# Constant multiplications on TensorE in front of waits, at the seams of stages and between the steps of the norms

## The chip, the cores and the metric

One core of a Trainium2 chip runs the whole program. TensorE multiplies, VectorE, ScalarE and GpSimd (POOL in the profile) do the elementwise work, SyncE issues the DMAs. The metric is the device time of one execution in microseconds; the time of a kernel is the median of its runs.

## The reference

Sequence 512, model width 1024, float32. Two different blocks follow each other, each two layers deep:

```python
# first block, hybrid layer
h = rms_norm(x, g_mix)
z = h @ w_in                                        # latents, conv input, queries, keys, values, gates
o_a = mla_mixer(...); o_b = conv_mixer(...); o_c = nsa_mixer(...)
g_a, g_b, g_c = split(sigmoid(gate_mix))
x = x + (g_a * o_a + g_b * o_b + g_c * o_c) @ w_out
x = x + square(relu(rms_norm(x, g_ffn) @ w_ff1)) @ w_ff2          # 4096 wide
# second block, layer; sh1, sc1, g1, sh2, sc2, g2 = split(c @ mod_w + mod_b)
h = rmsnorm(x, norm1_g) * (1 + sc1) + sh1
x = x + g1 * mixer(h)      # sparse (top-k) attention and forgetting attention, each gated, then @ w_out
h = rmsnorm(x, norm2_g) * (1 + sc2) + sh2
x = x + g2 * conv_ffn(h)   # up to 2 x 2816, causal 3-tap conv, silu(a) * b, down
# and a last rmsnorm of the result
```

All eight heads of each attention see all 512 tokens under their masks.

## The kernel before

Activations lie transposed: features on the 128 partitions, the 512 tokens along the row, eight such tiles for a width of 1024. A weight chunk is 128 x 1024 float32; SyncE streams all of them through a ring in the order of use.

**Products.** Every linear product is exact to about float32 by splitting both sides into a high and a low part (`w_hi`, `w_lo`, `a_hi`, `a_lo`) that TensorE takes in a faster format, and adding three passes in one PSUM bank: high x high, high x low, low x high (`split_pass` L265, `split_products` L278). A pass over one unit of 128 output features is eight matmuls of 512 columns. ScalarE makes the high part of a chunk of weights (`weights_hi` L190), GpSimd its low part (`weights_lo` L213). At the start of a stage the source tiles are cut as well: ScalarE makes `a_hi` tile by tile and counts them in `src_hi` (`split_source_hi` L236), VectorE makes `a_lo` and counts in `src_lo` (`split_source_lo` L247). The first unit of such a stage is given the tuple `fresh`: in its first pass TensorE waits for `src_hi` before each of the eight matmuls, then does low weights x high source, and in its last pass waits for `src_lo` before each.

**Stages.** The program is a sequence of stages (`stage` L101). Each is a block of five instruction programs, one for each engine, with a barrier at its end that all engines meet; semaphores of the stage order the work inside it. PSUM has 8 banks of 128 x 512; nothing in PSUM is carried through a stage's end but the scale that a norm leaves in bank 7. Layer by layer:

- first block: `norm_stage`, `first_front_stage` (L1232), `head_norm_stage` (L1090), `attention_stage` (latent attention), `compressed_attention_stage` (L1688), `attention_stage` (two branches in one), `gate_stage` (L1817), `merge_stage` (L967), `linear_stage` for the output projection, `norm_stage`, `linear_stage` for `ff_up`, `down_stage`;
- second block: `norm_stage`, `front_stage` (L2100), `attention_stage` twice (sparse, forgetting), `gate_stage`, `merge_stage`, `linear_stage` for the output projection, `norm_stage`, `gated_up_stage` (L2307), `down_stage`; a last `norm_stage` ends the program.

**The norm** (L668): TensorE adds the squares of the features by eight one-column matmuls (L704, two records for each of four token blocks), ScalarE and VectorE make the reciprocal root, VectorE puts it on a diagonal, and TensorE spreads that over all partitions (L708) into bank 7.

**`linear_stage`** (L415; TensorE's program L441 to L453): unit `g` goes to bank `g`; it waits for the bank's evacuation counter `act_evac` or `dve_evac`. With evacuation by ScalarE (`ff_up`, `body` 4) that counter gets its starting value from ScalarE's own queue, behind `split_source_hi`; with evacuation by VectorE (the output projections, `body` 8) VectorE gives it first of all. **`gated_up_stage`** has the same order with the counter `copied`. **`down_stage`** (L507) takes the hidden tiles two at a time, cuts them as it goes (`src_hi`, `src_lo`) and keeps eight banks of sums to its end.

**`attention_stage`** (L772): for each head ScalarE, VectorE and GpSimd make the softmax (scaling of the probabilities by GpSimd, L961) between TensorE's scores (L810, L811 adds the mask), transposes (L822) and products with the values (L833). Scores run one head ahead, products one behind. Parts of the gates' product are put between them (`Beside`, L354). `compressed_attention_stage` begins with 64 small score matmuls (L1756). `merge_stage` multiplies four source tiles of each branch (L1007).

TensorE's queue is in order. Its program of the first pass, with the waits of the first unit, is

```python
    for k in range(KD):
        if fresh and p != 1:
            pe.wait_ge(fresh[p // 2], k + 1)
        mm = m.nc.tensor.matmul(bank, unit_tile(w, k), a[:, k, :], ...)
```

## Time and profile before

| | |
|---|---|
| median of 3 runs | 3797.79 us (3797.69 to 3797.9) |
| the profiled execution, its own time | 3806.13 us |
| its span in the profile | 3804.4 us |
| mean granted clock of TensorE | 0.951 of full |
| TensorE (PE) busy | 3539.8 us, 93%, 16040 instructions |
| weight loads (PEld) | 2837.5 us, 75% |
| VectorE (DVE) | 2085.7 us, 55% |
| ScalarE (ACT) | 1381.2 us, 36% |
| GpSimd (POOL) | 1796.9 us, 47% |

The span is from the first to the last instruction that the profile has, the time includes what lies around it. The profiled execution was 8.3 us longer than the median. PE is the matmuls' own time, PEld the loads of the stationary operand, which overlap it. A timeline row groups like instructions that follow each other: start in us, busy time in us, engine, line, operation, output and inputs, rows*columns of the array, the moving operand's shape, the count; in brackets the idle time before it and the instruction that ended it. PEq, ACTq stand for an engine's queue, L107 and L122 for the barriers of stages. A float32 matmul has two records; the split formats have one. A clock of 0.50 is 1.2 GHz, 1.00 is 2.4 GHz.

### The profile page before, as it was taken

What the parts mean: (1) busy time and instruction counts of PE and PEld (TensorE: products, weight loads), DVE (VectorE), ACT (ScalarE), POOL (GpSimd) and SP (SyncE); (2) the same over time, 40 slices, a digit from 0 to 9 for tenths busy, and PEclk for the clock granted to TensorE, in tenths of its full rate; (3) what the DMA queues carried; (4) which work ended last, traced back from release to release, by engine and by line L of the source; (5) the groups of instructions that cost most, each with busy time, mean ns of one, the idle gap of its engine ahead of it and who ended that gap; (6) DMA issues with size and microseconds to landing.
All of it is one profiled execution on the core that took longest, in us unless ns stands there. A gap on an engine that the chain in (4) does not pass through costs nothing. (4 is left out here: it accounts for less than half of the span.)

```text
span 3804.4 us, 45924 instructions
## 1 busy us (share of the span) xinstructions
PE 3539.8 (93%) x16040; PEld 2837.5 (75%) x16040; DVE 2085.7 (55%) x3069; ACT 1381.2 (36%) x2431; POOL 1796.9 (47%) x1010
## 2 busy tenths in 40 slices
PE   7999999899999989989997999989999998989997
PEld 6866777787778667768786677778877676768876
DVE  5766645213367666551123575468864575558953
ACT  3243642322333436432223345333333345333332
POOL 3347844444344477434442466434543465434542
PEclk9998999999999989999998999989999999989998
DMA  4310023222232101223243220433333220533322
GB/s 154 102 51 28 29 78 111 83 94 90 87 123 96 33 28 38 86 94 99 99 141 103 67 72 23 166 117 111 126 139 117 67 67 23 180 108 116 121 88 88
DMA packets 95564, 346.56 MB, mean 91 GB/s; under 512 B 11440, under 2 KB 12080, under 8 KB 94768
## 3 DMA queue, kind: packets, MB, share of 16 engines
q1 hardware_dynamic: 95408, 344.54, 26.8%
q8 instruction: 90, 1.47, 0.2%
q14 instruction: 66, 0.54, 0.0%
HBM read 338.14 MB, written 6.29 MB: 91 GB/s over the span
## 5 line engine op out<-in xcount | busy, mean ns | idle before, releaser
L216 POOL TENSOR_TENSOR weights_lo<-arena,weights_hi 128x1024 fp32r<-128x1024 f32 x478 | 1209.0, 2530 | 1661.8 <-ACT weights_hi L200 1373.4
L200 ACT ACTIVATE weights_hi<-arena 128x1024 fp32r<-128x1024 f32 x489 | 515.5, 1054 | 648.9 <-PE ps L567 402.9
L274 PE MATMUL ps<-moving_hi,weights_hi 128*128 128x512 f32 x2448 | 648.5, 408 | 53.8 <-ACT moving_hi L242 18.9
L274 PE MATMUL ps<-moving_lo,weights_hi 128*128 128x512 f32 x2448 | 614.4, 393 | 3.7 <-DVE moving_lo L233 2.9
L274 PE MATMUL ps<-moving_hi,weights_lo 128*128 128x512 f32 x2448 | 613.9, 393 | 0.0
L274 PEld LDWEIGHTS ps<-moving_hi,weights_hi 128*128 128x128 f32 x2448 | 471.2, 194 | 179.3 <-issue 15.1
L274 PEld LDWEIGHTS ps<-moving_lo,weights_hi 128*128 128x128 f32 x2448 | 462.4, 189 | 109.6 <-DVE moving_lo L233 7.8
L274 PEld LDWEIGHTS ps<-moving_hi,weights_lo 128*128 128x128 f32 x2448 | 464.7, 190 | 105.4 <-issue 6.5
L961 POOL TENSOR_SCALAR arena<-arena 128x128 f32<-128x128 f32 (+1 forms) x320 | 349.2, 1109 | 199.8 <-DVE arena L875 163.1
L233 DVE TENSOR_TENSOR moving_lo<-arena,moving_hi 128x512 fp32r<-128x512 f32 x212 | 233.5, 1154 | 243.2 <-ACT moving_hi L228 243.2
L567 PE MATMUL ps<-moving_hi,weights_hi 128*128 128x512 f32 x864 | 217.1, 394 | 18.7 <-ACT moving_hi L228 18.7
L567 PE MATMUL ps<-moving_lo,weights_hi 128*128 128x512 f32 x864 | 217.2, 394 | 6.6 <-DVE moving_lo L233 6.6
L924 ACT ACTIVATE arena<-ps,arena 128x512 f32<-128x512 f32 (+1 forms) x320 | 164.8, 526 | 145.6 <-DVE arena L864 145.0
L567 PE MATMUL ps<-moving_hi,weights_lo 128*128 128x512 f32 x864 | 213.8, 390 | 0.0
L1950 DVE TENSOR_TENSOR arena<-arena x64 | 44.3, 692 | 301.8 <-ACT arena L1948 301.8
L567 PEld LDWEIGHTS ps<-moving_hi,weights_hi 128*128 128x128 f32 x864 | 164.0, 190 | 53.7 <-issue 19.6
L567 PEld LDWEIGHTS ps<-moving_lo,weights_hi 128*128 128x128 f32 x864 | 164.2, 190 | 42.4 <-DVE moving_lo L233 8.1
L567 PEld LDWEIGHTS ps<-moving_hi,weights_lo 128*128 128x128 f32 x864 | 162.8, 188 | 34.0
L2373 ACT ACTIVATE arena<-ps 128x512 f32<-128x512 f32 x88 | 52.8, 600 | 323.8 <-PE ps L274 323.8
L884 DVE TENSOR_TENSOR split<-ps,split 128x512 fp32r<-128x512 f32 (+1 forms) x240 | 129.8, 595 | 70.5 <-ACT split L946 70.1
L864 DVE TENSOR_REDUCE arena<-ps 128x1 f32<-128x512 f32 (+1 forms) x320 | 136.2, 481 | 53.1 <-PE ps L811 52.8
L833 PE MATMUL ps<-split,split 128*128 128x512 f32 (+3 forms) x640 | 125.9, 336 | 20.2 <-ACT split L946 19.7
(319 smaller groups left out, 4883.9 us busy)
## 6 DMA issues: line engine op xcount, KB each, us to landing
arena<-wstream SPq DMA_DIRECT2D x532, 512.0 KB, 3.3
arena<-modw SPq DMA_DIRECT2D x64, 512.0 KB, 3.7
arena<-modw_first SPq DMA_DIRECT2D x32, 512.0 KB, 4.1
layer_input<-arena SPq DMA_DIRECT2D x2, 2048.0 KB, 7.0
arena<-layer_input SPq DMA_DIRECT2D x2, 2048.0 KB, 8.3
arena<-xT SPq DMA_DIRECT2D x1, 2048.0 KB, 8.6
outT<-arena SPq DMA_DIRECT2D x1, 2048.0 KB, 7.0
arena<-con SPq DMA_DIRECT2D x1, 1411.5 KB, 11.0
```

The costliest lines, as they stand in the source:

```text
L200: m.nc.scalar.activation(m.w_hi[:, j % 2, :], slab(m, base + at), ACT.Copy).then_inc(hi_ready, 1)
L216: m.nc.gpsimd.tensor_tensor(m.w_lo[:, j % 2, :], slab(m, base + (j if at is None else at)), m.w_hi[:, j % 2, :].bitcast(F32), ALU.subtract)\
L233: return m.nc.vector.tensor_tensor(m.a_lo[:, k, :], tile, m.a_hi[:, k, :].bitcast(F32), ALU.subtract)
L274: mm = m.nc.tensor.matmul(bank, unit_tile(w, k), a[:, k, :], start=(p == 0 and k == 0), stop=(p == 2 and k == KD - 1))
L567: mm = nc.tensor.matmul(m.ps[:, 4 * half + n, :], unit_tile(w[:, j % 2, :], 2 * n + k), a[:, 2 * h + k, :], start=(first and p == 0 and k ...
L833: mm = nc.tensor.matmul(m.ps[:, 6, kt * P:T], values(j, b, kt), m.r(part)[:, PT_AT[kt]:PT_AT[kt] + T - kt * P], start=(b == 0 and p == 0 a ...
L864: r = nc.vector.tensor_reduce(mx[:, 4 * (u % 2) + qt:4 * (u % 2) + qt + 1], m.ps[:, bank, c:c + P * (qt + 1)], AX, ALU.max, negate=True)
L884: nc.vector.tensor_tensor(m.r(low)[:, at:at + w], m.ps[:, bank, 0:w], m.r(pt)[:, at:at + w].bitcast(F32), ALU.subtract)\
L924: a = nc.scalar.activation(prob[:, u % 2, PROB_AT[qt]:PROB_AT[qt] + P * (qt + 1)], m.ps[:, bank, c:c + P * (qt + 1)], ACT.Exp, bias=mx[:, ...
L961: r = nc.gpsimd.tensor_scalar(v, v, rinv[:, s + qt:s + qt + 1], None, ALU.mult)
L1950: post=lambda dve, n, *_: nc.vector.tensor_tensor(m.hidden[:, n, :], m.hidden[:, n, :], m.hidden[:, n, :], ALU.mult))
L2373: nc.scalar.activation(u[:, s, 2:W], m.ps[:, s, :], ACT.Copy).then_inc(copied, 1)
```

## The change

A helper multiplies the identity (128 x 128) with the first `width` columns of the constants that begin with it, in float32, and writes the result into a bank that nobody reads before it is written anew. It is called `count` times wherever the diff says. In the diff `T` is 512 and `P` 128. `fresh` gets a third item, the bank of these constants. Three loops have their first iteration unrolled, since only there `fresh` is given. Three stages' ends get a wait before their constants.

```diff
+def keep_busy(m, bank, count, width=T):
+    for _ in range(count):
+        m.nc.tensor.matmul(m.ps[:, bank, 0:width], m.con("ident", P), m.con("ident", width), start=True, stop=True)
 def split_pass(pe, m, base, i, j, body, bank, hi_ready, lo_ready, p, fresh=None):
     for k in range(KD):
         if fresh and p != 1:
+            if p == 0:
+                keep_busy(m, fresh[2], 1, 256)
             pe.wait_ge(fresh[p // 2], k + 1)
 # linear_stage
             pe.sem_inc(chunk_done, 1)
-            with loop(pe, iters) as i:
-                for g in range(body):
...
+            keep_busy(m, 5 if body < 6 else 7, 2)
+            def chunk(i, g, fresh):
+                who = evac[g][0]
+                pe.wait_ge(counters[who], i * len(mine[who]) + mine[who].index(g) + 1)
+                split_products(pe, m, base, i, g, body, m.ps[:, g, :], hi_ready, lo_ready, fresh).then_inc(chunk_done, 1)
+            for g in range(body):
+                chunk(0, g, (src_hi, src_lo, 5 if body < 6 else 7) if source and g == 0 else None)
+            if iters > 1:
+                with pe.Fori(1, iters) as i:
+                    for g in range(body):
+                        chunk(i, g, None)
             if tail:
                 pe.wait_ge(dve_evac, len(mine["dve"]) + 1)
                 tail[0](pe, *side)
+            elif body < 6:
+                keep_busy(m, 5, 2)
+            else:
+                pe.wait_ge(dve_evac, len(mine["dve"]) + 1)
+                keep_busy(m, 0, 2)
 # down_stage
                 for p, (w, a, ready) in enumerate(passes):
+                    if half == 0 and first and ready:
+                        keep_busy(m, 7, 2 + p)
                     if half == 0 and ready:
                         pe.wait_ge(ready, i * 4 + 2 * h + 2)
...
+            else:
+                pe.wait_ge(updated, 1)
+                keep_busy(m, 0, 6)
 # norm_stage
             mm.then_inc(summed, 1)
+            keep_busy(m, 2, 2)
             for t in range(TT):
                 pe.wait_ge(diag_done, t + 1)
...
             mm.then_inc(spread_done, 1)
+            keep_busy(m, 2, 1, 256)
 # attention_stage
+            keep_busy(m, 0, 3)
             product(NU - 1)
+            keep_busy(m, 0, 1)
 # merge_stage
                         for k in range(4):
+                            if b == 0 and j == 0 and ready:
+                                keep_busy(m, 7, 1, 256)
                             if j == 0 and ready:
                                 pe.wait_ge(ready, 4 * b + k + 1)
...
-            if modulate:
-                pe.wait_ge(gated, 8 * (NB - 1) + 2)
+            pe.wait_ge(gated, 8 * (NB - 1) + 2)
+            if not modulate:
+                keep_busy(m, 0, 3)
+            else:
 # head_norm_stage, end
+            keep_busy(m, 6, 2)
 # first_front_stage: start; its first unit has (src_hi, src_lo, 4); end
+            keep_busy(m, 4, 2)
...
+            pe.wait_ge(unit_squared, 10)
+            pe.wait_ge(k_out, 4)
+            keep_busy(m, 5, 2)
 # compressed_attention_stage: start; end
+            keep_busy(m, 6, 2)
...
+            keep_busy(m, 6, 1)
 # gate_stage: start; end
+            keep_busy(m, 0, 2)
...
+            pe.wait_ge(evaced, count - BANKS + 1)
+            keep_busy(m, count % BANKS, 1)
 # front_stage: start; its first unit has (src_hi, src_lo, 3)
+            keep_busy(m, 3, 2)
 # gated_up_stage: start; its first unit has (src_hi, src_lo, 6), iteration 0 is unrolled, the loop runs from 1 to 11
+            keep_busy(m, 6, 2)
```

## Rows read from the trace of the kernel before

**Rows 1.** Page: TensorE's granted clock in 40 slices, tenths of full speed
```profile
PEclk9998999999999989999998999989999999989998
```

**Rows 2.** Windows over low-clock stretches: length, PE PEld DVE ACT POOL, clock, DMA, GB/s
```profile
256.84:270.48 13.64, 13.63 (x32) 8.03 (x33) 4.62 (x11) 6.63 (x18) 6.73 (x7) 0.50 0.00 1
...
376.30:379.72 3.42, 3.42 (x13) 2.50 (x14) 1.32 (x3) 0.78 (x2) 0.00 (x0) 0.50 0.00 0
...
482.12:488.94 6.82, 5.82 (x14) 4.59 (x15) 4.39 (x4) 4.05 (x5) 4.77 (x2) 0.50 0.21 61
...
sum 376.20, PE 263.21 PEld 198.20 DVE 212.43 ACT 147.23 POOL 151.25; mean PE 6.93 PEld 5.22 DVE 5.59 ACT 3.87 POOL 3.98
```

**Rows 3.** Timeline of TensorE near 271 us: start, duration, operation, count, [idle before, releaser]
```profile
271.66 1.02 PE L810 MATMUL ps<-arena 96*128 96x512 f32 x2
272.52 0.22 PE L811 MATMUL ps<-arena 128*128 128x128 bf16 x1
```

**Rows 4.** Timeline of TensorE, norm and `ff_up` start of the first layer
```profile
668.71 1.02 PE L704 MATMUL ps<-arena 128*128 128x1 f32 x8 [2.44 <-PEq L107]
...
671.77 2.08 PE L708 MATMUL ps<-arena 128*128 128x128 f32 x8 [2.04 <-DVE arena L722]
...
679.64 3.78 PE L274 MATMUL ps<-moving_hi,weights_hi 128*128 128x512 f32 x8 [5.79 <-ACTq L461]
683.22 2.12 PE L274 MATMUL ps<-moving_hi,weights_lo 128*128 128x512 f32 x8
```

**Rows 5.** Timeline of TensorE, start of `gated_up_stage`
```profile
2556.17 3.78 PE L274 MATMUL ps<-moving_hi,weights_hi 128*128 128x512 f32 x8 [6.86 <-ACT moving_hi L242]
```

**Rows 6.** Timeline of TensorE, norm at the start of layer 1
```profile
1045.20 1.84 PE L704 MATMUL ps<-arena 128*128 128x1 f32 x8 [6.93 <-PEq L122]
```

**Rows 7.** Timeline, end of head norms and start of the first attention
```profile
229.29 0.63 PE L1185 MATMUL ps<-arena 128*37 128x128 f32 x4 [1.08 <-DVE arena L1166]
...
256.85 2.04 PE L810 MATMUL ps<-arena 96*128 96x512 f32 x2 [1.36 <-PEq L107]
...
263.75 4.27 POOL L961 TENSOR_SCALAR arena<-arena 128x128 f32<-128x128 f32 x4 [27.14 <-DVE arena L875]
...
270.57 1.25 PE L822 MATMUL ps<-arena 128*128 128x128 f32 x10
```

**Rows 8.** Timeline of TensorE, start of the forgetting attention
```profile
2329.16 1.03 PE L822 MATMUL ps<-arena 128*128 128x128 f32 x8
```

**Rows 9.** Timeline of TensorE, end of the sparse-branch attention, then gates
```profile
477.12 1.31 PE L822 MATMUL ps<-arena 128*128 128x128 f32 x10 [1.19 <-POOL arena L961]
479.23 1.75 PE L833 MATMUL ps<-split,split 128*128 128x512 f32 x8 [0.80 <-ACT split L946]
...
483.12 3.75 PE L274 MATMUL ps<-moving_hi,weights_hi 128*128 128x512 f32 x8 [2.15 <-ACTq L195]
...
489.57 2.00 PE L274 MATMUL ps<-moving_hi,weights_lo 128*128 128x512 f32 x8
```

**Rows 10.** Timeline of TensorE, compressed attention
```profile
324.58 13.03 PE L1756 MATMUL ps<-arena 64*128 64x31 f32 x64 [2.49 <-ACT arena L1729]
...
337.54 3.78 PE L354 MATMUL ps<-moving_hi,weights_hi 128*128 128x512 f32 x8
```

**Rows 11.** Timeline of TensorE, start of the merge, first layer
```profile
550.77 1.22 PE L1007 MATMUL ps<-moving_lo,weights_hi 128*128 128x512 f32 x2 [2.03 <-DVE moving_lo L233]
```

**Rows 12.** Timeline of TensorE, start of `down_stage`, first layer
```profile
859.01 2.06 PE L567 MATMUL ps<-moving_hi,weights_hi 128*128 128x512 f32 x8 [3.23 <-ACT moving_hi L228]
...
864.11 3.55 PE L567 MATMUL ps<-moving_lo,weights_hi 128*128 128x512 f32 x8 [3.04 <-DVE moving_lo L233]
```

**Rows 13.** Timeline of TensorE, start of `down_stage`, second layer
```profile
2805.82 3.75 PE L567 MATMUL ps<-moving_hi,weights_hi 128*128 128x512 f32 x8 [6.13 <-ACT moving_hi L228]
```

**Rows 14.** Timeline of TensorE, start of the output projection, second layer
```profile
2489.94 4.35 PE L274 MATMUL ps<-moving_hi,weights_hi 128*128 128x512 f32 x8 [1.60 <-ACT moving_hi L228]
```

**Rows 15.** Timeline of TensorE, start of the output projection, first layer
```profile
626.42 1.71 PE L274 MATMUL ps<-moving_lo,weights_hi 128*128 128x512 f32 x3 [0.95 <-DVE moving_lo L233]
```

More of the change, by code:

```diff
@@ L443, in _ @@
             pe.sem_inc(chunk_done, 1)
-            with loop(pe, iters) as i:
-                for g in range(body):
-                    who = evac[g][0]
-                    pe.wait_ge(counters[who], i * len(mine[who]) + mine[who].index(g) + 1)
-                    split_products(pe, m, base, i, g, body, m.ps[:, g, :], hi_ready, lo_ready,
-                                   (src_hi, src_lo) if source and g == 0 else None).then_inc(chunk_done, 1)
+            keep_busy(m, 5 if body < 6 else 7, 2)
[9 more added lines that the diff above has]
+                        chunk(i, g, None)
             if tail:
@@ L1313, in linear @@
                     free(n - 3)
-                split_products(pe, m, base, 0, n, count, bank(n), hi_ready, lo_ready, (src_hi, src_lo) if n == 0 else None)\
+                split_products(pe, m, base, 0, n, count, bank(n), hi_ready, lo_ready, (src_hi, src_lo, 4) if n == 0 else None)\
                     .then_inc(chunk_done, 1)
@@ L2180, in _ @@
                 for p in range(3):
-                    mm = split_pass(pe, m, base, 0, c, count, bank(c), hi_ready, lo_ready, p, (src_hi, src_lo) if c == 0 else None)
+                    mm = split_pass(pe, m, base, 0, c, count, bank(c), hi_ready, lo_ready, p, (src_hi, src_lo, 3) if c == 0 else None)
                     if p == 2:
@@ L2347, in _, with chunk @@
             pe.sem_inc(chunk_done, 1)
-            with pe.Fori(0, 11) as i:
+            keep_busy(m, 6, 2)
+            def chunk(i, s, fresh):
+                pe.wait_ge(copied, i * 4 + s + 1)
+                split_products(pe, m, base, i, s, 4, m.ps[:, s, :], hi_ready, lo_ready, fresh).then_inc(chunk_done, 1)
+            for s in range(4):
+                chunk(0, s, (src_hi, src_lo, 6) if s == 0 else None)
+            with pe.Fori(1, 11) as i:
                 for s in range(4):
-                    pe.wait_ge(copied, i * 4 + s + 1)
-                    split_products(pe, m, base, i, s, 4, m.ps[:, s, :], hi_ready, lo_ready,
-                                   (src_hi, src_lo) if s == 0 else None).then_inc(chunk_done, 1)
+                    chunk(i, s, None)
             pe.wait_ge(mod_added, KD + 1)
```

## Prediction, made before the changed kernel was run

> **What bounds the kernel now.** I read the slices of the page first, then the stretches in which the granted clock is low, then the timeline around each seam. The slices show TensorE near full and its clock in tenths mostly at 9 [rows 1]. The reader is to see in the second view why: the clock stands at 0.50 of full (1.2 GHz instead of 2.4) in 38 stretches, 376.20 us in sum, and TensorE is at work in 263.21 us of them [rows 2]. Work at half rate takes twice its time, so at most 263.21 / 2 = 131.6 us could come back, 3.5% of the span. That is the ceiling of any edit that only keeps the clock up. The timeline then shows what each seam waits for. Inside the stages TensorE runs product after product without a gap, so a microsecond added to its stream is added to the time, and one taken out of it comes back, except where another engine's chain is later.
>
> The Trainium skill (TensorE: Matmul & The Clock Gate, Part 1) says that the cost of the clock's ramp is under 1% of a typical kernel's span. By that the ceiling would be some 38 us, an estimate from that page; the trace disagrees with its 3.5%.
>
> **What the constants cost.** One constant multiplication of 512 columns is two passes in float32. Two such passes stand 0.86 us apart from the next instruction at 2.4 GHz [rows 3] and take about 1.7 at 1.2 GHz (2.04 with the drain, [rows 7]). One of 256 columns is taken as half, 0.43 (0.86 at the low clock); a product's matmul is 3.58 / 8 = 0.45 at the low clock [rows 4] and half of that at the high one. The queue of TensorE is in order: a constant ahead of a wait delays what is behind it by whatever it takes beyond the end of the wait. Constants at a stage's end delay the barrier only if they outlast the other engines.
>
> **Does a constant hold the clock?** No row shows one. Between float32 work that didn't raise it and work that did hold it: in an attention stage that starts low, TensorE is full from 256.84 to 270.48 and stays at 0.50 through all of its float32 scores of 96 rows [rows 2, 7]. On the other side the ten float32 transposes at 477.12, which use all 128 rows, come after 1.19 us of idle, another 0.80 follows, and no low stretch begins before 482.12 [rows 2, 9]. The constants use all 128 rows, as the transposes do, so I take it that they hold the clock across gaps that they mostly fill and raise it when they stand close together. The other answer is a rival below.
>
> **Gains, part by part.** The sum is made against the profiled execution (3806.13 us, span 3804.4), 8.3 us over the median of the runs shown; the difference is carried over to 3797.79.
> - Attention after the head norms, twice: the scores now start at the low clock, and the first transposes come at 270.57 [rows 7]. At the high clock two rounds of scores and one product take about 7 us instead of 13.7, but the transposes wait for Pool's scaling, which begins some 2 us after the first scores (263.75, with a 4.3 us run) [rows 7]: 2.5 + 2 + 4.5 = 9 us after the start, so TensorE waits 2 us. With 0.7 us for the two constants that end the stage before, later than VectorE, the gain is 13.7 − 9 − 0.7 = 4.0 each. The forgetting attention starts the same way, its transposes at 2329.16 [rows 8]: 3.4 each, after 1.0 for the constants before it. Sum −14.8.
> - Sparse-branch attention of the first layers, twice: its first 3.42 us are low [rows 2]; −1.5 each by the same chain, −3.0.
> - Merge: the low-part wait ends at 550.77 by VectorE, and then 8 + 2 matmuls run low [rows 11]: the half-width constants of the low pass lie inside that wait. −1.4, −1.4, −1.5, and +0.2 in the one merge that stays at the high clock: −4.1.
> - Down projection of the first layers, twice: both groups of constants lie in the 3.23 and 3.04 us of idle, and the low stretch that follows the second (8 matmuls in 3.4 us) goes [rows 12]: −1.7 each, −3.4.
> - The two norms behind the six constants: the column sums fall from 1.84 to 1.02 us [rows 4, 6], of which a table load of ScalarE keeps 0.2, the spreading from 2.08 to about 1.1, and 0.43 is given back by the constant before the barrier: −1.0 each, −2.0.
> - Compressed attention, twice: 64 small matmuls take 13.03 us low [rows 10], some 6.5 high, but they load the array so little that I expect the clock to fall within them: −3.9. Against it the three constants ahead of the last product of the attention before, at the low clock there, +2.1, and the two of the stage's start, +1.4: −0.4 each, −0.8.
>
> Gains: −28.1.
>
> **Costs.**
> - Up projections, four stages. Here `copied` or `act_evac` is given only after ScalarE has cut all eight sources, so the first matmul waits until 679.64 (idle 5.79, released by ACTq L461) [rows 4] and 2556.17 (idle 6.86) [rows 5]. The two constants ahead of that wait are free and leave over 3 us of idle, so the clock is low again at the end. The eight half-width constants come after that wait, and nothing covers them: 8 x 0.45 = 3.6, about 3.8 with the switches between kinds. With −0.4 for the norm before `ff_up` and +1.2 for the one before `gated_up`: 2 x 3.6 + 2 x 5.0 = +17.2 (rounded). This is the largest term.
> - Norms that are entered at the low clock (the first one, and the first of each second layer; those before `gated_up` stand above): two constants take 3.4 in a gap of 2.04 [rows 4], and the one behind comes before the barrier; the stage after gets its high clock sooner. +0.8, +0.9, +1.5: +3.2.
> - Gate stage, four times: three constants for a wait of 0.80 us and then the product at once, +1.1 to +1.3; two at the start, where TensorE waited for nothing but the barrier, +1.6. The first two products take 3.62 instead of 6.45 after the sparse branch (483.12 to 489.57) [rows 9]: −0.1 each; after the forgetting attention only 1.7 comes back: +1.0 each. Sum +1.8.
> - Output projection, four times: two constants and eight half-width ones beside a ScalarE pace of 0.52 us per source: 11.0 us of work from the barrier to the end of the first unit. In the first layers VectorE's low parts are late anyway (a wait of 0.95 us at 626.42) [rows 15], so only +0.6 is seen; in the second layers the clock is low at the start [rows 14]: +2.7 and +1.9. Sum +5.8.
> - Down projection of the second layers, started low [rows 13]: five constants against 2 us of cover: +2.5, +2.8.
> - Head norms, twice: the first product ends 1.7 us sooner, but the next step waits for VectorE until 229.29 [rows 7], and the longer idle (3 us) may lower the clock for what follows: +1.7 with a chance of 0.65, +1.1 each, +2.2.
>
> Costs: +35.5. Sum −28.1 + 35.5 = +7.4; 3797.8 + 7.4 = 3805.
>
> **Bounds.** For the hold of the clock: nothing of the gains (0), or the whole ceiling of rows 2. For a constant: 0.43 to 1.7 us. If the constants of the up projections were covered, 15 us of cost would go; what hides the others is named above, and without the cover of VectorE the merges and the first down projections would cost 1.4 and 2.6 each more. Where the gaps lie in time against the clock's changes moves each seam by up to 1.7 us either way; over some 40 seams that is about ±8.
>
> **Rivals.**
> - *The constants hold the clock better than taken, and it ends faster.* One mechanism: the clock is still high when the first pass of the up, output and second down projections begins, after an idle of 3 us with two constants in it. It decides at the nine starts of those stages. Each then saves the half of some 4 us, −17 in all, and the 64 small matmuls save their full 6.5 instead of 3.9, −5: 3805 − 22 = 3783. For it: idle of 3.04 us is needed before a low stretch in rows 12. Against it: the idle that is left is about as long. Chance 0.27.
> - *They don't hold or raise it*, as the 96-row float32 work didn't [rows 7]. Then the gains go and the costs stay: 3797.8 + 35.5 = 3833. For it the full 13 us of rows 7, against it the transposes of rows 9. The Trainium skill (TensorE: Matmul & The Clock Gate, Part 4) says that transposes don't count as busy for the clock in the same way; if so, this evidence for the forecast falls, and the page speaks for this rival; rows 9 disagree with it. Chance 0.15.
> - *Nothing comes of it*: idle of TensorE is idle of others, the constants vanish in the waits, and the clock falls at the same places because the long gaps have none in them. 3797.8 + 1 = 3799. Against it the up projections, whose wait is over before their constants. Chance 0.12.
>
> **How the numbers follow.** The forecast, 3805, has 0.46, with its own range from 3797 to 3814. About 0.2% (7.6 us) is what a measurement here tells from no change. Half of the forecast's case lies under it: same is 0.22 + 0.10 of the third rival, 0.32. Slower is 0.24 + 0.15 = 0.39, rounded to 0.40. Faster is 0.27 + 0.01 = 0.28. The range from 3780 to 3822 takes in the first and third rivals and leaves out the second and the far ends.
>
> **What would show it.** In the profile after: eight constants between the first eight product matmuls of each up projection, the first of these passes 3.5 to 4 us longer than now; the stretch of rows 2 at 256.84 gone and a wait for Pool of about 2 us in front of the first transposes; the column sums of the norm at 1.02 us; the sum of the low stretches at some 230 us instead of 376.20, but few of them gone where up, output and second down projections start. A low stretch that stays at 256.84 would speak for the second rival; high clock at the start of the up projections, for the first.

## The result, and the profile after

| | before | changed |
|---|---|---|
| median | 3797.85 us (3797.69 to 3804.81, 4 runs) | 3824.24 us (3821.7 to 3826.09, 4 runs) |
| profiled execution, span | 3804.4 us | 3823.1 us |
| mean granted clock | 0.951 | 0.977 |
| stretches at 1.2 GHz | 38, 376.20 us [rows 2] | 26, 175.16 us |
| TensorE busy | 3539.8 us | 3655.8 us; the constants' group 249.0 |

The ratio of the two is 1.0063, 95% interval 1.0048 to 1.0079: the changed kernel is slower by 0.6%. Run once more beside the experiments it gave 1.0068 (1.0054 to 1.0082). Forecast were 3805 us and a range from 3780 to 3822; the ratio puts the time at 3821.7, 0.3 us inside the range's upper edge, and the kernel's own median is 2 us above it. That it falls inside is luck: by the ratio of the second measurement it would be 3823.6, outside. The sign was right and the size wrong: +7.4 was forecast, +19 is what the two profiled executions differ by, +24 to +26 the runs.

The page of the changed kernel, TensorE's own lines (the first engine row, the granted clock by slices, and the groups at the constants' line L268; for the groups: count, busy us, mean ns, idle before). The clock row answers to [rows 1].

```profile
PE 3655.8 (96%) x16606; PEld 2895.6 (76%) x16606; DVE 2081.9 (54%) x3069; ACT 1381.5 (36%) x2431; POOL 1797.2 (47%) x1010
...
PEclk9998999999999989999998999999999999999999
...
L268 PE MATMUL ps<-arena 128*128 128x512 f32 (+1 forms) x566 | 249.0, 550 | 44.5 <-ACTq L195 14.0
```

The windows over the low stretches of the changed kernel, first all of TensorE's work, the sum that answers to that of [rows 2], then the constants' own part in the same windows:

```profile
sum 175.16, PE 131.43 PEld 95.73 DVE 96.37 ACT 51.36 POOL 59.50; mean PE 5.05 PEld 3.68 DVE 3.71 ACT 1.98 POOL 2.29
...
sum 175.16, PE 55.20 PEld 24.97; mean PE 2.12 PEld 0.96
```

With these the account of TensorE's span closes. The kernel's own work at 1.2 GHz fell from 263.21 us to 131.43 − 55.20 = 76.2, which is worth (263.2 − 76.2) / 2 = 93.5 us, seven tenths of the forecast's ceiling. Idle time fell from 3804.4 − 3539.8 = 264.6 to 3823.1 − 3655.8 = 167.3, 97.3 less. Busy time rose by 116.0, so the constants put 116.0 + 93.5 = 209.5 us into TensorE's stream (their group has 249.0, since the recorded ends of matmuls overlap what follows). −93.5 − 97.3 + 209.5 = +18.7, the difference of the spans. The constants do hold the clock, and more than was forecast (175 us of low stretches instead of some 230). But only 97 us of them lie in idle time, and the other 112 are dearer than the 93.5 that the clock gives.

The start of an up stage in the changed kernel, TensorE's timeline (start us, busy us, line, count, idle before). It answers to the norm and `ff_up` rows of [rows 4]:

```profile
666.70 1.02 PE L727 MATMUL ps<-arena 128*128 128x1 f32 x8 [0.73 <-PEq L107]
667.59 1.96 PE L268 MATMUL ps<-arena 128*128 128x512 f32 x4
669.76 1.16 PE L732 MATMUL ps<-arena 128*128 128x128 f32 x8 [0.21 <-DVE arena L747]
670.76 0.60 PE L268 MATMUL ps<-arena 128*128 128x256 f32 x2
671.80 1.95 PE L268 MATMUL ps<-arena 128*128 128x512 f32 x4 [0.45 <-PEq L107]
677.12 0.70 PE L268 MATMUL ps<-arena 128*128 128x256 f32 x2 [3.36 <-ACTq L479]
...
679.33 0.99 PE L282 MATMUL ps<-moving_hi,weights_hi 128*128 128x512 f32 x1
680.11 1.05 PE L268 MATMUL ps<-arena 128*128 128x256 f32 x2
680.61 0.99 PE L282 MATMUL ps<-moving_hi,weights_hi 128*128 128x512 f32 x1
...
684.16 2.01 PE L282 MATMUL ps<-moving_hi,weights_lo 128*128 128x512 f32 x8
```

The reader is to see that between the norm's steps the two constants fill the gap (0.21 us of it is left), that TensorE still idles for 3.36 us ahead of the counter that ScalarE gives, and that only then come the half-width constants. The first pass with them takes 684.16 − 677.12 = 7.04 us; it took 3.58 (679.64 to 683.22).

The attention behind the head norms, TensorE's timeline; [rows 7] had 256.85 to 270.57 at 1.2 GHz here:

```profile
260.84 1.10 PE L835 MATMUL ps<-arena 96*128 96x512 f32 x2 [0.45 <-PEq L107]
...
266.64 2.09 PE L362 MATMUL ps<-moving_hi,weights_hi 128*128 128x512 f32 x8
270.02 1.31 PE L847 MATMUL ps<-arena 128*128 128x128 f32 x10 [1.29 <-POOL arena L988]
```

From the first score to the first transpose it takes 9.2 us instead of 13.7, and the wait for GpSimd's scaling is there, 1.29 us.

The seam to the forgetting attention, TensorE's timeline:

```profile
2302.76 2.24 PE L847 MATMUL ps<-arena 128*128 128x128 f32 x10 [0.71 <-POOL arena L988]
2304.79 3.54 PE L268 MATMUL ps<-arena 128*128 128x512 f32 x6
2307.76 1.80 PE L858 MATMUL ps<-split,split 128*128 128x512 f32 x8
2309.40 1.07 PE L268 MATMUL ps<-arena 128*128 128x512 f32 x2
...
2329.44 2.13 PE L362 MATMUL ps<-moving_hi,weights_lo 128*128 128x512 f32 x8 [1.57 <-POOL weights_lo L346]
```

Three constants take 3 us here, in front of a product that waited 0.83 us before, and 1.6 us of what the scores save (4.5 us) ends in a wait for a low part of weights that GpSimd makes behind its scaling.

### The profile page after: what moved, and what is told of

The parts are those of the page before. It is cut to its first block and busy times, and to the rows that moved or that the text cites. A ratio compares the mean times of both kernels' runs of the same rounds, so it can differ in the third digit from the quotient of the medians.

```text
span 3823.1 us, 47022 instructions
## 1 busy us (share of the span) xinstructions
PE 3655.8 (96%) x16606; PEld 2895.6 (76%) x16606; DVE 2081.9 (54%) x3069; ACT 1381.5 (36%) x2431; POOL 1797.2 (47%) x1010
## 5 line engine op out<-in xcount | busy, mean ns | idle before, releaser
L282 PE MATMUL ps<-moving_lo,weights_hi 128*128 128x512 f32 x2448 | 607.2, 390 | 0.0
L282 PEld LDWEIGHTS ps<-moving_hi,weights_hi 128*128 128x128 f32 x2448 | 459.2, 189 | 107.5 <-issue 13.9
L268 PE MATMUL ps<-arena 128*128 128x512 f32 (+1 forms) x566 | 249.0, 550 | 44.5 <-ACTq L195 14.0
L587 PE MATMUL ps<-moving_lo,weights_hi 128*128 128x512 f32 x864 | 214.5, 390 | 0.0
L268 PEld LDWEIGHTS ps<-arena 128*128 128x128 f32 x566 | 113.3, 211 | 125.3 <-issue 75.8
L587 PEld LDWEIGHTS ps<-moving_hi,weights_hi 128*128 128x128 f32 x864 | 163.6, 189 | 36.9 <-issue 2.0
## 6 DMA issues: line engine op xcount, KB each, us to landing
arena<-con SPq DMA_DIRECT2D x1, 1411.5 KB, 11.3
```

The lines of the kernel that those rows point to most:

```text
L268: m.nc.tensor.matmul(m.ps[:, bank, 0:width], m.con("ident", P), m.con("ident", width), start=True, stop=True)
L282: mm = m.nc.tensor.matmul(bank, unit_tile(w, k), a[:, k, :], start=(p == 0 and k == 0), stop=(p == 2 and k == KD - 1))
L587: mm = nc.tensor.matmul(m.ps[:, 4 * half + n, :], unit_tile(w[:, j % 2, :], 2 * n + k), a[:, 2 * h + k, :], start=(first and p == 0 and k ...
```

## The experiments

All ratios are to the kernel before on the same chip, with their 95% interval. The low stretches are summed over each one's own profiled execution; one and the same program differs in them from one execution to the next. The runs were made on several chips, so two variants are compared by way of their ratios.

| run | ratio | interval | low stretches, us |
|---|---|---|---|
| changed kernel | 1.0063, 1.0068 | 1.0048 to 1.0079, 1.0054 to 1.0082 | 175 |
| no constants | 0.9998 | 0.999 to 1.0007 | 342 |
| no half-width ones in first units | 0.9991 | 0.9982 to 0.9999 | 164 |
| 64 rows | 1.0548 | 1.0531 to 1.0564 | 504 |
| five ahead of the up stages' wait | 0.9984 | 0.9975 to 0.9993 | 151 |
| ... in the first block only | 0.9971 | 0.9962 to 0.9981 | 260 |
| ... in the second block only | 1.0039 | 1.0026 to 1.0053 | 278 |
| no half-width ones in up stages | 1.0016 | 1.0007 to 1.0025 | 168 |
| none in the norms | 1.0042 | 1.0029 to 1.0056 | 189 |
| none at starts and ends of front, output, gate stages | 1.0036 | 1.0022 to 1.0049 | 199 |
| selected sites | 0.9932 | 0.9919 to 0.9946 | 206 |
| selected sites and more | 0.9918 | 0.9904 to 0.9932 | 187 |

**No constants, the structure stays.**

```diff
 def keep_busy(m, bank, count, width=T):
-    for _ in range(count):
+    for _ in range(0):
```

> All constant multiplications left out; the unrolled first iterations and the added waits at the ends of stages stay. My theory (the constants themselves are the cost): the time of the kernel before, 3798, within 2 us, and again some 376 us at 1.2 GHz. Rival (the unrolled loops' longer programs or the waits at the stages' ends cost the 26 us, the constants are paid for by the clock): 3815 to 3825.

Measured 0.9998. The unrolled iterations and the added waits cost nothing that shows; what the change costs is in the constants. The low stretches sum to 342 us and not to some 376: this execution took 3797.43 us, at the fast end of the kernel before's own spread, and its mean granted clock was 0.955 instead of 0.951.

**No half-width constants in first units.**

```diff
-            if p == 0:
+            if False:
                 keep_busy(m, fresh[2], 1, 256)
```

> The changed kernel without the half-width constants in the first pass of a stage's first unit (front, output projection and up stages; the merge keeps its own). My theory: 3 us back in each of the four up stages, where they stand behind the wait that ends the idle time, 1 to 2 in the output projections of the second layers, and about 1 lost again at each of the four front stages, where the clock falls again: 13 us less than the changed kernel, about 3811, still slower than before. Rival (they pay for themselves by the clock): no less than the changed kernel, 3822 to 3830.

Measured 0.9991, 0.7% or 27 us below the changed kernel and not 13. With these 96 constants the low stretches sum to 175 us, without them to 164: they buy no clock at all. In the first layer's `ff_up` the first unit even runs at 2.4 GHz without them, after the same 3.36 us of idle time; TensorE's timeline of that run:

```profile
670.01 1.95 PE L268 MATMUL ps<-arena 128*128 128x512 f32 x4 [0.45 <-PEq L107]
675.32 2.11 PE L282 MATMUL ps<-moving_hi,weights_hi 128*128 128x512 f32 x8 [3.36 <-ACTq L479]
677.27 1.98 PE L282 MATMUL ps<-moving_hi,weights_lo 128*128 128x512 f32 x8
```

**64 rows instead of 128.**

```diff
-m.con("ident", P), m.con("ident", width)
+m.con("ident", P)[0:64, :], m.con("ident", width)[0:64, :]
```

> The changed kernel with the constants' products over 64 rows of the array instead of 128 (same columns, same number). My theory (the clock counts how much of the array works, as the 96-row scores at 1.2 GHz suggested): the constants hold little of the clock, the low stretches sum to over 250 us, and the constants that run at the low clock cost twice: 3840 to 3880. Rival (the clock only sees that TensorE is busy): the time and the 160 us of low stretches of the changed kernel, 3824.

Measured 1.0548, far beyond the range. The low stretches sum to 504 us, more than the 342 to 376 without any constants. The windows' sum and TensorE's timeline in the same up stage:

```profile
sum 504.24, PE 444.61 PEld 251.57 DVE 216.63 ACT 114.77 POOL 157.27; mean PE 15.88 PEld 8.98 DVE 7.74 ACT 4.10 POOL 5.62
```

```profile
709.06 1.22 PE L268 MATMUL ps<-arena 64*128 64x256 f32 x2
710.21 0.79 PE L282 MATMUL ps<-moving_hi,weights_hi 128*128 128x512 f32 x1
710.93 1.22 PE L268 MATMUL ps<-arena 64*128 64x256 f32 x2
712.08 0.79 PE L282 MATMUL ps<-moving_hi,weights_hi 128*128 128x512 f32 x1
```

A constant and a product take 710.93 − 709.06 = 1.87 us here, at 1.2 GHz; in the changed kernel, at 1.2 GHz too, 680.61 − 679.33 = 1.28 (the rows above). So two things make up the 190 us: the clock, and some 0.6 us for each alternation between 64 and 128 rows. The constants are at work in 212 of the 444.61 us of TensorE's work at the low clock; the kernel's own work there is 232 us, 156 more than in the changed kernel, which is worth 78 us. The rest is the constants' own time. In the long stretches the clock stays at 1.2 GHz while TensorE is busy: this one lasts from 695.79 to 726.51, into the third pass of the first unit.

Whether the clock counts rows is not settled by it. At other seams the constants of 64 rows did what those of 128 do: with two of them at the end of the head norms the attention starts at 2.4 GHz, and its low stretch of 13.6 us [rows 2] is gone; so are those at the start of the first block's down projections. TensorE's timeline at the first of these seams:

```profile
270.76 1.96 PE L268 MATMUL ps<-arena 64*128 64x512 f32 x4
273.17 1.10 PE L835 MATMUL ps<-arena 96*128 96x512 f32 x2 [0.45 <-PEq L107]
```

The run changes two things at once where constants stand between products: the rows, and the 0.6 us that each alternation adds. None here changes one without the other.

**Five constants ahead of the wait of the up stages.**

```diff
-            keep_busy(m, 5 if body < 6 else 7, 2)
+            keep_busy(m, 5 if body < 6 else 7, 2 + 3 * (body < 6))
...
-            keep_busy(m, 6, 2)
+            keep_busy(m, 6, 5)
```

> As the run without the half-width constants, and five full-width constants instead of two at the start of the four up stages, ahead of the wait that leaves TensorE idle for 3.4 to 5 us. My theory: five fit into that idle time at 2.4 GHz (4.3 us) and the first unit then runs at 2.4 GHz, 1.7 us less for each stage: 7 less than that run, about 3804. Rival (the clock falls anyway, or the constants outlast the wait): the same as that run or up to 4 us more.

Measured 0.9984, where 0.9991 was the run without the move: 3 us, half of what was expected, and the two intervals overlap. In the first `ff_up` there was nothing left to win: the first pass takes 2.11 us in both runs, after 3.36 us of idle time (the row at 675.32 above) and after 0.79:

```profile
676.17 2.11 PE L282 MATMUL ps<-moving_hi,weights_hi 128*128 128x512 f32 x8 [0.79 <-ACTq L479]
```

**Which block.** The helper does nothing in the second block, or in the first:

```diff
-    for _ in range(count):
+    for _ in range(0 if m.stream_base else count):
```

> As the run with five constants moved to the start of the up stages, with constants in the first block alone. Its trace is 17 us ahead of the kernel before at the end of the first block and gives 8 back in the second. Theory A (each site has its own worth: constants pay where the clock would fall in a gap they fill, and cost where a stage is entered at 1.2 GHz or TensorE isn't idle): 12 to 15 us faster than the kernel before, ratio 0.996 to 0.997. Theory B (the worth of a site is where the gaps happen to lie against the clock's changes, which shifts with all that is ahead): no different from that run, 0.998 to 0.999.

> The complement: the same constants in the second block alone. Theory A: 6 to 9 us slower than the kernel before, ratio 1.0015 to 1.0025, and the two halves' differences add up to that of the run with both. Theory B: within 3 us of the kernel before, and they don't add up.

Measured 0.9971 and 1.0039. The signs are theory A's, the first block gains and the second loses. The sizes are neither's: they add to +0.10%, and the run with both is at −0.16%, a difference of 10 us. That is above the three intervals taken together as independent errors (0.19%), though not above their plain sum, and the run with both was on another chip: it suggests that what is ahead of a site moves its worth, which the run without half-width constants in the up stages, below, shows in its trace.

**The changed kernel again**, beside these three:

> The changed kernel once more, on one chip with the runs that are compared with it. Every theory expects the same ratio to the kernel before, 1.005 to 1.008; it gives the differences between the variants on one chip.

**Three groups taken out of the changed kernel, one at a time.**

```diff
# up stages
-            if p == 0:
+            if p == 0 and fresh[2] is not None:
                 keep_busy(m, fresh[2], 1, 256)
...
-                chunk(0, g, (src_hi, src_lo, 5 if body < 6 else 7) if source and g == 0 else None)
+                chunk(0, g, (src_hi, src_lo, None if body < 6 else 7) if source and g == 0 else None)
...
-                chunk(0, s, (src_hi, src_lo, 6) if s == 0 else None)
+                chunk(0, s, (src_hi, src_lo, None) if s == 0 else None)
# norms
-            keep_busy(m, 2, 2)
...
-            keep_busy(m, 2, 1, 256)
# edges: start and end of the output projections, of the first front stage and of the gate stages; start of the second block's front stages
-            keep_busy(m, 5 if body < 6 else 7, 2)
+            if body < 6: keep_busy(m, 5, 2)
...
-                keep_busy(m, 0, 2)
...
-            keep_busy(m, 4, 2)
...
-            keep_busy(m, 5, 2)
...
-            keep_busy(m, 0, 2)
...
-            keep_busy(m, count % BANKS, 1)
...
-            keep_busy(m, 3, 2)
```

> The changed kernel without the half-width constants in the four up stages only; everything else as changed. It sizes the largest term of the forecast (8 x 0.45 = 3.6 us for each stage, 14.4 in all). Theory A (they only cost their own time): 14 us less than the changed kernel, ratio to it 0.9963. Theory B (where they straddle a fall of the clock they cost twice their time, and the first unit would mostly start at 2.4 GHz without them): 17 to 20 us less, ratio 0.995.

Measured 1.0016, 0.5% or some 19 us below the changed kernel. In the two profiled executions the four up stages are shorter by 3.5, 3.5, 3.6 and 3.6 us, 14.2 in all; the forecast had 14.4. A further 2.9 in the profiles came in the forgetting attention (1.8) and the output projection (1.2) of the second block's first layer, where nothing was changed. Neither theory is quite it: own time in the stage, and a shift of what follows.

> The changed kernel without the constants of the nine norms. Forecast's terms: -2.0 for the two norms behind the six constants, +3.2 and +1.6 for the others, so 3 us less than the changed kernel without them, ratio 0.999. Rival (they carry the clock over the barrier into the stage after, which is worth more than they cost): 3 us or more above the changed kernel.

Measured 1.0042, some 9 us below the changed kernel by the runs and 5 by the two profiles (3818.3 against 3823.1 us of span). The norms' constants cost 5 to 9 us and not 3, though its interval overlaps a little with the changed kernel's; the rival is refuted.

> The changed kernel without the full-width constants at the starts of front, output and gate stages and at the ends of the front, output and gate stages (the waits there stay, and so do the half-width ones). Theory A (a stage's start has no idle time for them and the clock gives part back): two constants of 0.86 us at twelve starts and one to two at eight ends, less some clock, 6 to 12 us less than the changed kernel, ratio 0.997 to 0.9985. Rival (the clock pays for them): the same as the changed kernel or above.

Measured 1.0036, some 11 us below by the runs, 6 by the profiles (3816.7 us of span): the two ends of theory A's range.

**Selected sites.** The diff against the changed kernel (where a line is only taken out it stands with a minus):

```diff
-                keep_busy(m, fresh[2], 1, 256)
-            keep_busy(m, 5 if body < 6 else 7, 2)
+            if body < 6: keep_busy(m, 5, 5)          # ff_up
# ends of ff_up and of the output projections
-                keep_busy(m, 5, 2)
-                keep_busy(m, 0, 2)
# down_stage, end of merge and of gate stage: in the first block only
-            keep_busy(m, 2, 2)
+            keep_busy(m, 2, 1)                        # norm
-            keep_busy(m, 2, 1, 256)
-            keep_busy(m, 0, 3)
+            keep_busy(m, 0, 1)                        # attention, ahead of the last product
-            keep_busy(m, 6, 2)
+            keep_busy(m, 6, 1)                        # compressed attention, start
# start of gate_stage and front_stage
-            keep_busy(m, 0, 2)
...
-            keep_busy(m, 3, 2)
-            keep_busy(m, 6, 2)
+            keep_busy(m, 6, 4)                        # gated_up_stage, ahead of the wait
```

> Constants only where the traces so far show them covered or repaid: one full-width constant between the norm's steps (it fits the 2.0 us gap at either clock), five at the start of ff_up and four of gated_up ahead of the wait, two at the end of the head norms, one before and one after the last product of an attention stage, the merges' own, and in the first block the down projections', the gates' last and the merge's last; nothing at starts of front, gate and output stages. Theory A: at least as good as the first block alone, 13 to 18 us faster than the kernel before, ratio 0.995 to 0.9965. Theory B: 0.998 or more.

The edit left the two constants at the start and the two at the end of `first_front_stage` in place, though "nothing at starts of front" stages was meant.

Measured 0.9932, 26 us faster than the kernel before, better than expected. It has more low stretches than the changed kernel (206 against 175 us) and is 51 us faster: the mean clock isn't the aim. Some ten sites differ at once, so the gain isn't told apart by site. TensorE's timeline at the start of its first `gated_up_stage` (answers to [rows 5], whose first pass took 3.78):

```profile
2513.96 2.05 PE L268 MATMUL ps<-arena 128*128 128x512 f32 x2
2515.94 2.07 PE L732 MATMUL ps<-arena 128*128 128x128 f32 x8
2518.48 5.57 PE L268 MATMUL ps<-arena 128*128 128x512 f32 x8 [0.47 <-PEq L107]
2524.87 2.11 PE L282 MATMUL ps<-moving_hi,weights_hi 128*128 128x512 f32 x8 [0.81 <-ACTq L2407]
```

**Selected sites and more.** Added to the version before:

```diff
                 j = 2 * h + half
+                if first and half == 0 and m.stream_base:
+                    keep_busy(m, 7, 3)
                 pe.wait_ge(hi_ready, i * 4 + j + 1)
...
     def sum_modulation(pe, squared, added, mod_added, mod_summed):
+        keep_busy(m, 0, 2)
         pe.wait_ge(mod_added, KD)
```

> The selected version (0.9932 of the kernel before), and besides: three constants at the start of the second block's down projections, ahead of the wait for the first weights, where TensorE is idle for 6.1 us and two passes at 1.2 GHz follow; two in the 2.1 us of idle time before the sum of the modulation at the end of its output projections. Theory A (what fits into idle time pays): 2 to 4 us faster than the selected version in each of the down projections, 0.5 to 2 in the others, ratio to the kernel before 0.991 to 0.992. Theory B (the clock's changes fall elsewhere and nothing is left over): 0.993 to 0.994.

Measured 0.9918, the fastest of all: 3772.03 us beside 3803.95, some 31 us. The interval overlaps with the version before. TensorE's timeline at the down projection of the second block's first layer, first of the version before, then of this one:

```profile
2776.13 3.75 PE L587 MATMUL ps<-moving_hi,weights_hi 128*128 128x512 f32 x8 [6.12 <-ACT moving_hi L228]
2780.40 3.78 PE L587 MATMUL ps<-moving_lo,weights_hi 128*128 128x512 f32 x8 [0.52 <-DVE moving_lo L233]
```

```profile
2771.09 4.25 PE L268 MATMUL ps<-arena 128*128 128x512 f32 x6 [4.94 <-PEq L107]
2774.78 2.41 PE L589 MATMUL ps<-moving_hi,weights_hi 128*128 128x512 f32 x8
2777.03 1.98 PE L589 MATMUL ps<-moving_lo,weights_hi 128*128 128x512 f32 x8
```

Both passes now run at 2.4 GHz, and from the first product on 4.4 us are saved to the stage's end. But the products begin as soon as the constants end: these began at 1.2 GHz, took 4.25 us, and outlasted the wait by 2.5 us (10.5 us from the last row of the stage before instead of 8.0), so 1.9 is left. The reason stands in the bracket: 4.94 of the 6.12 us of idle time lie ahead of the barrier (PEq L107), where a constant of this stage can't go, and only 1.2 behind it. In the second layer it is +3.3 and −1.7: nothing is won there. Theory A's 2 to 4 us for each is refuted; between the two versions' profiles most of the gain (4.5 us) lies from the second block's first modulation sum to the up stage behind it: 0.7 up to the first product of the up stage, 2.2 in its third pass, where waits for VectorE's low parts are gone, and 1.6 in the pass after it, now at 2.4 GHz. Why those waits went was not traced.

The account of this version closes as that of the changed kernel did. Its sums over the low stretches, all of TensorE's work and then the constants' part:

```profile
sum 187.44, PE 135.50 PEld 99.60 DVE 110.09 ACT 58.75 POOL 79.06; mean PE 5.42 PEld 3.98 DVE 4.40 ACT 2.35 POOL 3.16
...
sum 187.44, PE 35.52 PEld 14.63; mean PE 1.42 PEld 0.59
```

Its own work at 1.2 GHz is 100.0 us, which gives (263.2 − 100.0) / 2 = 81.6 us. Busy time is 3583.0, 43.2 above the kernel before, so the constants put 43.2 + 81.6 = 124.8 us into the stream; idle time is 184.7, 79.9 less. Only 44.9 us of constants lie outside idle time, against 112 in the changed kernel, for most of the gain by the clock (81.6 against 93.5): −81.6 − 79.9 + 124.8 = −36.7, the difference of the spans (3767.7 against 3804.4).

## Why the prediction was right or wrong

Positions of the same matmuls in the two profiled executions give each seam's share. Forecast and measured, in us, in the order of the kernel's layers:

| step of the forecast | forecast | measured |
|---|---|---|
| four up stages with their norms | +17.2 | +3.2, +3.1, +4.6, +5.6 = +16.5 |
| down projections, first block | −3.4 | −1.8, −1.8 |
| down projections, second block | +5.3 | +2.9, +3.7 |
| compressed attention | −0.8 | −0.5, −0.7 |
| attention after the head norms | −8.0 | −3.5, −3.5 |
| forgetting attention with the end ahead of it | −6.8 | −0.2, −0.6 |
| sparse-branch attention | −3.0 | −0.5, −0.1 |
| gates with the attention's end | +1.8 | +0.2, −0.5, +1.4, +2.9 |
| merges and output projections | +1.7 | −0.7, −0.7, +1.0, +0.5 |
| the rest (other norms, fronts, head norms) | +3.4 | +4.7 |
| sum | +7.4 | +18.7 |

**Bounds and ceiling.** Right: no more than 131.6 us could come back, and some 93.5 did, with 175 us of low stretches left where the forecast had some 230. It came at 112 us of constants outside idle time.

**Do the constants hold the clock?** Right: 175 us low with them, 342 without, and the second rival is refuted. The reason given, that they use all 128 rows, is shown in part at most: over 64 rows the sum was 504 us (+5.5%), but at the end of the head norms and in the first block's down projections 64 rows held the clock as well.

**Up stages.** Right to 1 us, the largest term of all: eight constants behind the wait that they should have lain in. The recorded sum has a slip of 0.2 in two of its terms (3.8 − 0.4 is 3.4, not 3.6), too small to matter.

**The step that failed** is "the forgetting attention starts the same way ... 3.4 each, after 1.0 for the constants before it". The scores gave what was counted on, 4.5 and 4.8 us in the two layers. The 1.0 was mis-sized: the attention's end has three constants ahead of the last product and one behind it, and in the first of these layers the clock is low when they begin. Up to that product they cost 2.3 us there and 1.9 in the second layer: the matmuls before it are 4.37 us earlier than in the kernel before, this product only 2.03 (2307.76 against 2309.80). And a wait was put at nothing: 1.7 to 1.8 us of the scores' gain went into the wait for `weights_lo`, made by GpSimd, which the forecast had looked for only at the scaling. That leaves 0.2 and 0.6 us. The same end of an attention stage stands before the gates, and start constants stand before the sparse branch; together with the forgetting attention these are 10.6 of the 11.3 us that the sum was short of the profiles (6.0, 2.2 and 2.4). The other steps miss by up to 1.6 us each, in both directions, and nearly cancel; that is luck. No run takes this step's constants out by themselves: its sizes are read from the two traces.

**The remaining 6 us** are between the profiled pair (+18.7) and the runs (+24 to +26). The profiled execution of before took 3806.13 us, 8.3 above its median, and the kernel before spread from 3795.0 to 3809.7 in the later runs. The first-block version spread over 14 us (3784.64 to 3798.45) as one and the same program. The time goes with the clock: of the 29 runs of the kernel before beside the first experiments, the fastest (3795.0 us) had a mean granted clock of 0.955 and the slowest (3809.56) one of 0.946; those of the first-block version had 0.970 and 0.966. So where the gaps fall against the clock's changes differs from one execution to the next, and the profiled execution of before, with 0.951 and 3806.13 us, is in the slower half of that spread. What sets it was not found.

**Rivals.** The first (the clock is still high when the up, output and second down projections begin) doesn't happen in the changed kernel, whose half-width constants begin at 677.12 at 2.4 GHz and run into 1.2. It can happen without them: 2.11 us for the first pass at 675.32. But after the same 3.36 us of idle time the version without half-width constants in the up stages alone took 2.54 us for that pass and 3.18 for the next, across a fall of the clock:

```profile
676.79 2.54 PE L282 MATMUL ps<-moving_hi,weights_hi 128*128 128x512 f32 x8 [3.36 <-ACTq L479]
679.13 3.18 PE L282 MATMUL ps<-moving_hi,weights_lo 128*128 128x512 f32 x8
```

So the idle time of one gap doesn't decide it, neither here nor as the prediction read it from [rows 12]. The third rival, nothing comes of it, is refuted by the 93.5 us that came back.

The Trainium skill (TensorE: Matmul & The Clock Gate, Part 1) puts the penalty of the clock's ramp below 1% of a typical span. Here the trace disagrees: 3.5% was lost at the low clock, since the clock falls again at the seams. The best version got 0.8% of it in time.

## What to carry to other kernels

Filling a gap with constants paid here ahead of the wait that makes the gap, and only as many as fit; behind the wait each costs its whole time (14.2 us for the 32 of the up stages), and all together more than the clock gave back. Place by place the trace before gives a safe count: idle time between the stage's barrier and the first matmul, divided by 1.7 us (512 columns in float32 at 1.2 GHz). Idle time ahead of the barrier doesn't count: three constants put against 6.12 us of idle, 4.94 of it ahead of the barrier, came 2.5 us late. A higher mean clock is no measure: 0.977 was slower than 0.951, and the best version had 0.975 at some 55 us less than the changed one.

## What the runs showed of the hardware

The same 283 constant multiplications took the low stretches from 342 us (none) to 175 us with 128 rows, and to 504 us with 64. With 64 rows the clock stayed at 1.2 GHz in stretches of 30.7 us, with TensorE busy for 28.7 of them, where constants stood between products; ahead of the attention 64 rows kept 2.4 GHz as 128 did. Alternating matmuls of 64 and of 128 rows cost some 0.6 us for each pair at 1.2 GHz. The same seam with the same 3.36 us of idle time was followed by 2.4 GHz in one version and by a fall to 1.2 in another. Programs longer by some unrolled iterations cost nothing that shows (0.9998).
